# Both mixers of a two-layer encoder: the order of gate chunks, pooled maps and decay sums rearranged

## The chip, the cores and the metric

One core of one Trainium2 chip runs the kernel. The metric is the device time of one execution in microseconds; the number that is predicted is the median over several runs.

## What is computed

Two layers, 256 tokens of width 1024, all in float32. Each layer has a mixer, an output projection, a layer norm, a channel mixer (dense SwiGLU in layer 0; top 2 of 8 experts in layer 1) and a second norm. The part that the change touches is the mixer, cut here to what matters:

```python
z = x @ w_in                     # pool 512 | q 512 | k 512 | v 512 | o 512 | gates 8
y_pool = pool_mixer(u_pool, ...) # trailing means over 2, 4, 8, 16 tokens minus the token; a 128x128 map per group
q, k = causal_conv_silu(qk)      # 4 taps
Dlog = b[t] - b[s] + ig[s]       # causal; b = cumsum(log_sigmoid(f))
m_t  = max(max_s Dlog, inter)
W    = exp(Dlog - m_t) * (q . k) * Dh**-0.5
num  = W @ v ;  den = sum_s W
h    = num / max(|den|, exp(-m_t))
h    = (h - mean) * rsqrt(var + eps)       # per head
y_m  = sigmoid(o_pre) * h * g
mix  = concat(y_pool, y_m) @ w_out
x    = layer_norm(ALPHA * x + mix)
```

The kernel computes the four heads over all 256 tokens at once, without the reference's chunks of 64.

## The kernel before

TensorE's exactness is bought by splitting. Each weight unit of 128x2048 (1 MB) arrives in `raw` by a DMA of SP's queue, ScalarE rounds it to float32r (`w_hi`, four buffers, `round_hi`, L824), VectorE subtracts (`w_lo`, three buffers, `subtract_lo`, L1172), and each product is three float32r matmuls, high by high, high by low and low by high (`product`, L1739 to L1741). Small matmuls (scores, sums, maps, transposes) are plain float32; the profile shows each such matmul as two records. A mixer has 14 units: v0 v1 q0 q1 k0 k1 p0 p1 o0 o1 (halves of the input projection, p for pool and o for the output gate) and w0 to w3 (`w_out`). Units of the mixer are numbered u0 to u13 here in that order. A helper called `ahead()` stands between the steps of ScalarE and of VectorE and does the next unit there; unit n can only be rounded when TensorE is through with unit n-4 and subtracted when it is through with unit n-3.

The order of each engine is written out by hand; nothing reorders it.

- TensorE (`mixer`, L1772 on): values, gates, chunks of q, of k, transposes of the gate rows (L1837), four broadcasts of the row of maxima to 128 partitions (L1840: a selector of 4x128 against `r_negm` of 4x256), p0 and p1, the scores (L1852 and L1853), o0, then the row sums of the decay weights W as matmuls with a column of ones (L1863, 12 matmuls of one column), the products of W with v (L1868, 12 matmuls of 128 columns; called PV here), pooled maps 0 and 1 (`pool_maps(0)`, L1877), o1, a wait for all four sigmoids, `pool_maps(1)` (L1877 again), `project(0, 0)` and `project(0, 1)` (the first quarter of the output projection for tokens 0 to 127 and 128 to 255; 12 matmuls of 512 columns each), eight transposes of the normed heads (L1913), and the other quarters for the first tokens and then for the second.
- The scores wait for all arguments of the exponentials (`arg_ready`), since their banks hold the broadcasts until then. PV waits for `w_ready`, four masked and multiplied W.
- ScalarE (L858 on): bias and gate functions, copies of q and k to SBUF (L874), eight SiLUs (L885), four exponentials (L907), `guard` (L909), u10, the four copies of the pool chunks to `ubuf` (L915), u11, u12 (which waits for the end of o0), rounding of the pooled outputs (`y_round`, L920), sigmoids of o (L926), standard deviations (L929).
- VectorE (L1201 on): v copies, the gate rows, convolutions (L1247, L1249), arguments of the exponentials (L1277, L1278), u9 has its subtraction here, then u10, then the four products W (L1286), u11, denominators (L1295 to L1299), `pooled(0)` (L1305), `head_stats(0)`, `y_low(0)`, `head_stats(1)`, `pooled(1)`, the two normings with a reciprocal each (L1344, L1346), `y_low(1)`, u12, eight products with the sigmoids (L1355), `y_low(2)` (L1316), u13, `y_low(3)`.
- GpSimd, called POOL: two of the eight convolutions, the causal mask on the exponentials (`masks`, L776), then the pooling of groups 0 to 3 (`pooling`, L733 to L749: g0 to g3 here).
- PSUM banks: pool and gate chunks use 0 to 3, so a chunk of o0 may start when ScalarE has copied the pool chunk out of its bank. PV uses banks 7 and 6, the sums 4; the projection sums into 0, 1, 4 and 5.

The lines of the code stand here as the profile counts them.

Of the kernel before, what the change touches and what calls it, by code (L numbers as in the profile page):

```python
# [7 lines left out]
F32 = mybir.dt.float32  # L8
# [205 lines left out]
def build(nc, x, w_in, b_gates, conv_w, conv_b, pool_w, pool_scale, mlstm_g, w_out, ln1_g, ln1_b, ln2_g, ln2_b,  # L214
          wg_dense, wu_dense, wd_dense, w_router, b_router, wg_exp, wu_exp, wd_exp, consts, out):
    with ExitStack() as ctx:
# [42 lines left out]
        def carve(shape, start=None):  # L259
            if start is not None:  # L260
# [23 lines left out]
        v_sb = carve([TT, D_MLSTM])  # L284
# [9 lines left out]
        rows = carve([5, T])  # L294
        qkT = carve([8, T])
        yT = qkT
        r_i, r_f, r_l, r_negm, r_m = (rows[0:HEADS, n, :] for n in range(5))
# [107 lines left out]
            ypool_ready, rden_ready, hvar_ready, h_ready, ym_ready, ylo_ready, var_ready, xhat_ready, dh_ready, \  # L405
# [3 lines left out]
                "cols_ready", "arg_ready", "w_ready", "ypool_ready", "rden_ready", "hvar_ready", "h_ready",  # L409
# [8 lines left out]
        shift_ready, turn_go = map(sem, ("shift_ready", "turn_go"))  # L418
# [36 lines left out]
        PV_BANKS = (7, 6)  # L455
        POOL_BANKS = (5, 2)
# [242 lines left out]
        def _(pool):  # L699
# [31 lines left out]
            def pooling(l):  # L731

                st.then(g.memset(ptmp[:, :, 0:16], 0.0))  # L733
                for gr in range(GROUPS):
# [45 lines left out]
            for l in range(LAYERS):  # L780
                convs(l)
                masks(l)
                pooling(l)
# [12 lines left out]
        def _(act):  # L796
# [61 lines left out]
            def mixer(l):  # L858
# [31 lines left out]
                copies("q", 0)  # L890
                if l:
                    act.wait_ge(tokens_ready, TT * 2)
# [11 lines left out]
                silu(3)  # L904
                for h in range(HEADS):
# [243 lines left out]
        def _(dve):  # L1149
# [51 lines left out]
            def mixer(l):  # L1201
                ahead()
                for t in range(TT):
                    dve.wait_ge(*chunk_event(l, "v", t))
                    v.tensor_copy(v_sb[:, t, :], bank[t][:, :]).then_inc(v_ready, 1)
# [22 lines left out]
                st.add(v.tensor_scalar(r_negm, r_m, -1.0, None, ALU.mult))  # L1228
                st.wait()
# [62 lines left out]
                dve.wait_ge(pv_mm, TT * l + 1)  # L1292
                den = bank[4][:, 0:TT * HEADS]
                rd, gd = (w[:].rearrange("p t h -> p (t h)") for w in (rden, guard))
                st.then(v.tensor_tensor(rd, den, gd, ALU.max))  # L1295
# [1009 lines left out]
```

## Time and profile before

| | before |
|---|---|
| median of 3 runs | 1341.83 us (1340.31 to 1342.46) |
| the profiled execution | 1338.05 us |
| its span | 1336.2 us |
| PE busy | 1278.6 us (96%) |
| PE weight load busy | 1044.5 us (78%) |
| DVE busy | 1126.5 us (84%) |
| ACT busy | 928.8 us (70%) |
| POOL busy | 89.3 us (7%) |
| mean granted clock of PE | 0.984 |

PE is TensorE, DVE is VectorE, ACT is ScalarE, POOL is GpSimd, SP is SyncE, which issues the weight loads. All times inside a trace count from the start of its span. The granted clock is a share of 2.4 GHz. The busy time of matmuls overlaps with the next one's (they are pipelined), so the distance from one start to the next says more than the length of one. The first mixer lies at 12 to 110 us, the dense part behind it up to about 310 us, the second mixer at 310 to 410 us, the routing of the experts at 410 to 440 us, and the experts behind it.

### The profile page before, as it was taken

How to read it: one execution, taken by the hardware profiler on the slowest of the kernel's cores; microseconds unless marked ns; L12 is line 12 of the kernel's file. 1: busy time of each engine (PE TensorE's matmuls, PEld its weight loads, DVE VectorE, ACT ScalarE, POOL GpSimd, SP SyncE). 2: the span in 40 equal slices, each digit the busy share in tenths (PEclk: the TensorE clock that was granted, in tenths of full speed). 3: DMA queues.
4: the chain of work that ended last, by engine and by line, in shares of the span. 5: the costliest groups of instructions: out<-in, count | busy, mean ns of one | idle time of the engine just before them, and what ended most of it. 6: DMA issues, size and time to landing. Idle time of an engine off the chain costs nothing.

```text
span 1336.2 us, 17022 instructions
## 1 busy us (share of the span) xinstructions
PE 1278.6 (96%) x6176; PEld 1044.5 (78%) x6176; DVE 1126.5 (84%) x931; ACT 928.8 (70%) x745; POOL 89.3 (7%) x111
## 2 busy tenths in 40 slices
PE   7999999999997989999999999999999999999996
PEld 5997888888986768777877777777777787677774
DVE  5868644458968799999998999879899989899997
ACT  5645444445534688888886888878778888788883
POOL 1550000000740000000000000000000000000000
PEclk9999999999996999999999999999999999999998
DMA  9637555544442999999999999999999999999992
GB/s 321 217 105 247 193 188 189 190 157 158 157 142 81 345 377 387 389 400 403 409 408 409 389 410 395 407 399 409 347 367 408 396 409 409 409 399 393 398 406 105
DMA packets 133053, 425.18 MB, mean 318 GB/s; under 512 B 9008, under 2 KB 11344, under 8 KB 132960
## 3 DMA queue, kind: packets, MB, share of 16 engines
q1 hardware_dynamic: 131600, 420.21, 82.8%
q0 software_dynamic: 1216, 3.71, 0.9%
q8 instruction: 53, 0.87, 0.3%
q14 instruction: 40, 0.33, 0.1%
q10 hardware_dynamic: 144, 0.07, 0.0%
HBM read 422.91 MB, written 1.05 MB: 317 GB/s over the span
## 4 chain that ended last, share of the span: by engine, by line
PE 76%; DVE 14%; issue 6%; ACT 3%; DMA 0%; DVEq 0%; ACTq 0%
PE bank L1739 19%; PE bank L1741 18%; PE bank L1740 18%; DVE w_lo L1158 7%; PE bank L2060 6%; PE bank L2061 6%; DVE w_lo L1172 2%; PE bank L2106 1%; PE bank L2093 1%; PE bank L2019 1%; PE bank L2034 1%; PE bank L2056 1%; PE bank L2057 1%; ACT w_hi L824 1%; DVE arena L1249 1%
## 5 line engine op out<-in xcount | busy, mean ns | idle before, releaser
L1158 DVE TENSOR_TENSOR w_lo<-raw,w_hi 128x2048 fp32r<-128x2048 f32 x216 | 485.9, 2285 | 32.8 <-PE bank L1741 18.8
L809 ACT CAST w_hi<-raw 128x2048 fp32r<-128x2048 f32 x216 | 407.5, 1915 | 67.8 <-PE bank L1741 66.6
L1739 PE MATMUL bank<-w_hi,parts 128*128 128x512 f32 x824 | 330.3, 401 | 13.5 <-issue 5.7
L1741 PE MATMUL bank<-w_hi,parts 128*128 128x512 f32 x824 | 322.7, 392 | 0.0
L1740 PE MATMUL bank<-w_lo,parts 128*128 128x512 f32 x824 | 322.4, 391 | 0.0
L2060 PE MATMUL bank<-w_hi,parts 128*128 128x512 f32 x672 | 270.0, 402 | 9.0 <-ACT arena L1024 3.1
L2061 PE MATMUL bank<-w_lo,parts 128*128 128x512 f32 x672 | 262.5, 391 | 0.0
L1739 PEld LDWEIGHTS bank<-w_hi,parts 128*128 128x128 f32 x824 | 155.6, 189 | 55.9 <-issue 15.2
L1172 DVE TENSOR_TENSOR w_lo<-raw,w_hi 128x2048 fp32r<-128x2048 f32 x61 | 140.3, 2303 | 62.7 <-PE bank L1741 51.7
L1158 DVE TENSOR_TENSOR w_lo<-arena,w_hi 128x2048 fp32r<-128x2048 f32 x80 | 181.2, 2285 | 10.6 <-ACT w_hi L809 8.5
L1741 PEld LDWEIGHTS bank<-w_hi,parts 128*128 128x128 f32 x824 | 155.5, 189 | 33.5
L1740 PEld LDWEIGHTS bank<-w_lo,parts 128*128 128x128 f32 x824 | 155.9, 189 | 30.9 <-issue 0.7
L824 ACT CAST w_hi<-raw 128x2048 fp32r<-128x2048 f32 x61 | 116.2, 1910 | 80.6 <-PE bank L1741 72.0
L2060 PEld LDWEIGHTS bank<-w_hi,parts 128*128 128x128 f32 x672 | 126.1, 188 | 53.9 <-DVE w_lo L1158 23.0
L809 ACT CAST w_hi<-arena 128x2048 fp32r<-128x2048 f32 x80 | 150.9, 1913 | 16.1 <-PE bank L2061 12.5
L2061 PEld LDWEIGHTS bank<-w_lo,parts 128*128 128x128 f32 x672 | 126.3, 188 | 25.1 <-issue 0.7
L1158 DVE TENSOR_TENSOR w_lo<-tokens,w_hi 128x2048 fp32r<-128x2048 f32 x40 | 91.4, 2285 | 2.8 <-ACT w_hi L809 2.3
L1739 PE MATMUL bank<-w_hi,x_hi 128*128 128x512 f32 (+1 forms) x224 | 85.3, 381 | 4.1 <-DVE w_lo L1172 4.0
L1741 PE MATMUL bank<-w_hi,x_lo 128*128 128x512 f32 (+1 forms) x224 | 84.8, 378 | 0.0
L1740 PE MATMUL bank<-w_lo,x_hi 128*128 128x512 f32 (+1 forms) x224 | 84.7, 378 | 0.0
L809 ACT CAST w_hi<-tokens 128x2048 fp32r<-128x2048 f32 x40 | 76.9, 1923 | 6.0 <-issue 4.3
L1739 PE MATMUL bank<-x_hi,w_hi 128*128 128x256 f32 x256 | 73.4, 287 | 0.4 <-ACT arena L915 0.4
(251 smaller groups left out, 1267.1 us busy)
## 6 DMA issues: line engine op xcount, KB each, us to landing
raw<-in_wu_exp SPq DMA_DIRECT2D x76, 1024.0 KB, 10.2
raw<-in_wg_exp SPq DMA_DIRECT2D x70, 1024.0 KB, 10.2
raw<-in_wd_exp SPq DMA_DIRECT2D x70, 1024.0 KB, 10.6
arena<-in_wd_exp SPq DMA_DIRECT2D x29, 1024.0 KB, 10.6
arena<-in_wg_exp SPq DMA_DIRECT2D x26, 1024.0 KB, 11.2
arena<-in_wu_exp SPq DMA_DIRECT2D x25, 1024.0 KB, 8.8
raw<-in_w_in SPq DMA_DIRECT2D x20, 1024.0 KB, 5.9
tokens<-in_wg_exp SPq DMA_DIRECT2D x16, 1024.0 KB, 11.8
```

What stands on the lines that cost most here:

```text
L809: a.copy(to, ring[s]).then_inc(hi_ready, 1)
L824: a.copy(w_hi[:, n % HIGH, :], raw[:, n % RAW, :]).then_inc(hi_ready, 1)
L1158: v.tensor_tensor(low(n), ring[s], high(n).bitcast(F32), ALU.subtract).then_inc(lo_ready, 1)
L1172: v.tensor_tensor(w_lo[:, n % SPLIT, :], raw[:, n % RAW, :], w_hi[:, n % HIGH, :].bitcast(F32), ALU.subtract).then_inc(lo_ready, 1)
L1249: ins = v.scalar_tensor_tensor(out=acc, in0=zqk[:, c, j:j + T], scalar=par_col(("conv_w", j), l, c), in1=acc, op0=ALU.mult, op1=ALU.add)
L1739: mm(psum, left[0], right[0], start=first, stop=False)
L1740: mm(psum, left[0], right[1], start=False, stop=False)
L1741: return mm(psum, left[1], right[0], start=False, stop=last)
L2019: last = mm(psum[:, at_c:at_c + width], parts_[:, t, k * P:(k + 1) * P], picks[:, t, :], start=t == 0, stop=t == TT - 1)
L2034: last = mm(bank[n][:, kk * BOTH:(kk + 1) * BOTH], parts_[:, t, k * P:(k + 1) * P], pick_both[:, t, :], start=t == 0, stop=t == TT - 1)
L2060: mm(psum, left, right[0], start=first, stop=False)
L2061: return mm(psum, left, right[1], start=False, stop=last)
```

## The change

Six edits, all in the mixers, in both layers.

1. The column of ones goes into `v_sb`: each head's v is 129 columns wide, the last one ones. The 12 one-column matmuls (L1863) are gone; the 12 PV matmuls have 129 columns and give sums beside the products. Three heads of a token tile lie in bank 7 or 6, the fourth head of both tiles in bank 4 (`head_sums`). The denominators are now read from three places, so their two VectorE operations become six, and they wait for all of PV. The wait of the projection for `rden_ready` becomes one for `hvar_ready`, put ahead of `project(0, 1)`.
2. The negated maxima are written as two float32r rows (`negm_hi`, `negm_lo`) with one more VectorE operation; the broadcast is two float32r matmuls for each head instead of one float32 matmul. ScalarE rounds the selector once (`head_sel`) in layer 0, after the copies of q.
3. TensorE runs chunks 0 and 1 of o0 before the scores, chunks 2 and 3 after them.
4. ScalarE copies pool chunks 0 to 2 before the exponentials, the last one after `guard`, and u10 comes after that one.
5. POOL runs g0 before the masks, g1 to g3 after them.
6. TensorE runs `pool_maps(1)` between `project(0, 0)` and `project(0, 1)`, and VectorE runs `pooled(1)` between the two normings instead of before both.

```diff
@@ buffers
-        v_sb = carve([TT, D_MLSTM])
+        v_sb = carve([TT, HEADS, DH + 1])
...
-        rows = carve([5, T])
+        rows = carve([4, T])
...
+        head_sel = parts[0:HEADS, 4096:4096 + HEADS * P]
+        negm_hi, negm_lo = (parts[0:HEADS, 4096 + HEADS * P + n * T:][:, 0:T] for n in range(2))
...
+        def head_sums(t, h):
+            b, c = (PV_BANKS[t], h) if h < HEADS - 1 else (4, t)
+            return bank[b][:, c * (DH + 1):(c + 1) * (DH + 1)]
@@ GpSimd
                 convs(l)
+                pooling(l, range(0, 1))
                 masks(l)
-                pooling(l)
+                pooling(l, range(1, GROUPS))
@@ ScalarE
                 copies("q", 0)
+                if l == 0:
+                    act.wait_ge(consts_in, 16)
+                    a.copy(head_sel, cst[0:HEADS, C_SEL:C_SEL + HEADS * P]).then_inc(sel_ready, 1)
...
                 silu(3)
+                act.wait_ge(qk_ready, 8 * (l + 1))
+                for c in range(GROUPS - 1):
+                    pool_input(c)
                 for h in range(HEADS):
                     act.wait_ge(arg_ready, HEADS * l + h + 1)
                     a.activation(decay[:, h, :], decay[:, h, :], ACT.Exp).then_inc(decay_ready, 1)
...
+                pool_input(GROUPS - 1)
                 ahead()
-                act.wait_ge(qk_ready, 8 * (l + 1))
-                for c in range(GROUPS):
-                    act.wait_ge(*chunk_event(l, "p", c))
-                    a.copy(ubuf[:, c, 16:], bank[c][:, 0:T]).then_inc(u_ready, 1)
                 ahead()
                 ahead()
@@ VectorE
+                    if t == 0:
+                        v.memset(v_sb[:, :, :, DH:DH + 1], 1.0).then_inc(vones_ready, 1)
...
-                st.add(v.tensor_scalar(r_negm, r_m, -1.0, None, ALU.mult))
-                st.wait()
+                st.then(v.tensor_scalar(negm_hi, r_m, -1.0, None, ALU.mult))
+                st.then(v.scalar_tensor_tensor(out=negm_lo, in0=r_m, scalar=-1.0, in1=negm_hi.bitcast(F32),
+                                               op0=ALU.mult, op1=ALU.subtract))
...
-                dve.wait_ge(pv_mm, TT * l + 1)
-                den = bank[4][:, 0:TT * HEADS]
...
+                dve.wait_ge(pv_mm, TT * (l + 1))
...
+                for rd_, gd, den in dens:
+                    st.add(v.tensor_tensor(rd_, den, gd, ALU.max))
+                st.wait()
+                for rd_, gd, den in dens:
+                    st.add(v.scalar_tensor_tensor(out=rd_, in0=den, scalar=-1.0, in1=rd_, op0=ALU.mult, op1=ALU.max))
+                st.wait()
...
                 head_stats(1)
-                pooled(1)
                 for t in range(TT):
...
+                    if t == 0:
+                        pooled(1)
@@ TensorE
+                pe.wait_ge(sel_ready, 1)
                 pe.wait_ge(rows_ready, l + 1)
...
-                    last = mm(bank[(7, 4)[h // 2]][:, (h % 2) * T:(h % 2 + 1) * T],
-                              cst[0:HEADS, C_SEL + h * P:C_SEL + (h + 1) * P], r_negm, start=True, stop=True)
+                    row = bank[(7, 4)[h // 2]][:, (h % 2) * T:(h % 2 + 1) * T]
+                    mm(row, head_sel[:, h * P:(h + 1) * P], negm_hi, start=True, stop=False)
+                    last = mm(row, head_sel[:, h * P:(h + 1) * P], negm_lo, start=False, stop=True)
...
                 chunks("p", 1)
+                chunks("o", 0, lambda c: (u_ready, GROUPS * l + c + 1), range(0, 2))
...
-                chunks("o", 0, lambda c: (u_ready, GROUPS * l + c + 1))
+                chunks("o", 0, lambda c: (u_ready, GROUPS * l + c + 1), range(2, 4))
...
-                for t in range(TT):
-                    for h in range(HEADS):
-                        for w, s in wts[t][h]:
-                            mm(bank[4][:, t * HEADS + h:t * HEADS + h + 1], w, ones[:, 0:1],
-                               start=s == 0, stop=s == t)
...
-                            last = mm(bank[PV_BANKS[t]][:, h * DH:(h + 1) * DH], w, v_sb[:, s, h * DH:(h + 1) * DH],
-                                      start=s == 0, stop=s == t)
+                            last = mm(head_sums(t, h), w, v_sb[:, s, h, :], start=s == 0, stop=s == t)
...
                 pe.wait_ge(sig_ready, HEADS * (l + 1))
-                pool_maps(1)
...
-                pe.wait_ge(rden_ready, l + 1)
                 arrived(mixer_unit(l, "w", 0))
                 project(0, 0)
+                pool_maps(1)
                 pe.wait_ge(ypool_ready, 2 * l + 1)
+                pe.wait_ge(hvar_ready, TT * (l + 1))
                 project(0, 1)
```

## Rows read from the trace of the kernel before

**Rows 1.** The page's part 4: the chain that ended last, shares of the span by engine.

```profile
PE 76%; DVE 14%; issue 6%; ACT 3%; DMA 0%; DVEq 0%; ACTq 0%
```

**Rows 2.** PE in stretches: bounds, length, busy (instructions), granted clock, DMA share, GB/s.

```profile
56.20:67.70 11.50, 11.50 (x96) 1.00 0.28 93
...
110.00:320.00 210.00, 206.43 (x998) 1.00 0.56 184
...
500.00:800.00 300.00, 295.64 (x1315) 1.00 1.02 400
```

**Rows 3.** PE timeline, first mixer: start us, us, engine, line, output<-inputs, count [idle<-releaser].

```profile
54.23 1.97 PE L1840 MATMUL bank<-arena,cst 4*128 4x256 f32 x8
...
67.75 0.59 PE L1852 MATMUL bank<-arena 128*128 128x256 f32 x2
...
76.11 2.74 PE L1863 MATMUL bank<-cst,arena 128*128 128x1 f32 x24
...
78.71 4.55 PE L1868 MATMUL bank<-arena 128*128 128x128 f32 x24
...
83.10 1.03 PE L1877 MATMUL bank<-arena,pool_ws 128*128 128x256 f32 x4
...
90.35 1.13 PE L1877 MATMUL bank<-arena,pool_ws 128*128 128x256 f32 x4 [0.47 <-ACT arena L926]
...
100.49 0.47 PE L1739 MATMUL bank<-w_hi,parts 128*128 128x512 f32 x1
```

**Rows 4.** PE timeline, second mixer, the same columns.

```profile
361.05 0.67 PE L1852 MATMUL bank<-arena 128*128 128x256 f32 x2 [1.67 <-DVE arena L1278]
...
377.09 1.03 PE L1877 MATMUL bank<-arena,pool_ws 128*128 128x256 f32 x4
```

**Rows 5.** PE in short stretches, columns of Rows 2.

```profile
78.00:79.00 1.00, 1.00 (x10) 1.00 0.03 8
...
80.00:81.00 1.00, 1.00 (x6) 0.50 0.73 119
...
26.50:30.00 3.50, 3.50 (x33) 1.00 1.05 390
...
414.00:418.00 4.00, 2.97 (x13) 0.52 0.01 2
```

**Rows 6.** DVE timeline, both mixers, columns of Rows 3.

```profile
65.33 2.29 DVE L1172 TENSOR_TENSOR w_lo<-raw,w_hi 128x2048 fp32r<-128x2048 f32 x1
...
68.55 2.29 DVE L1172 TENSOR_TENSOR w_lo<-raw,w_hi 128x2048 fp32r<-128x2048 f32 x1 [0.94 <-ACT w_hi L824]
...
70.77 1.94 DVE L1286 SCALAR_TENSOR_TENSOR arena<-bank,arena 128x384 f32<-128x384 f32 x4
...
91.52 0.88 DVE L1305 TENSOR_SCALAR arena<-bank,par 128x256 f32<-128x256 f32 x2 [0.84 <-PE bank L1877]
...
360.81 2.28 DVE L1172 TENSOR_TENSOR w_lo<-raw,w_hi 128x2048 fp32r<-128x2048 f32 x1
```

**Rows 7.** ACT timeline, both mixers, the same columns.

```profile
63.56 1.28 ACT L907 ACT_TABLE_LOAD   x1
...
64.85 1.76 ACT L907 ACTIVATE arena<-arena 128x384 f32<-128x384 f32 x4
...
68.42 1.17 ACT L915 COPY arena<-bank 128x256 f32<-128x256 f32 x4
...
358.00 0.91 ACT L885 ACTIVATE arena<-arena,par 128x256 f32<-128x256 f32 x2 [1.82 <-DVE arena L1249]
```

**Rows 8.** POOL timeline, first mixer, the same columns.

```profile
66.75 1.94 POOL L776 TENSOR_SCALAR_AFFINE_SELECT arena<-arena 128x512 f32<-128x512 f32 x2 [5.49 <-ACT arena L907]
...
69.10 2.22 POOL L744 TENSOR_TENSOR arena<-arena 128x256 f32<-128x256 f32 x1
...
73.54 1.31 POOL L744 TENSOR_TENSOR arena<-arena 128x256 f32<-128x256 f32 x2
...
76.02 0.72 POOL L749 TENSOR_TENSOR arena<-arena 128x256 f32<-128x256 f32 x1
```

More of the change, by code:

```diff
@@ L293, in build @@
         ln_rows = {1: ln_old, 2: ln_mid, 3: ln_new}
-        rows = carve([5, T])
+        rows = carve([4, T])
         qkT = carve([8, T])
         yT = qkT
-        r_i, r_f, r_l, r_negm, r_m = (rows[0:HEADS, n, :] for n in range(5))
+        r_i, r_f, r_l, r_m = (rows[0:HEADS, n, :] for n in range(4))
+        head_sel = parts[0:HEADS, 4096:4096 + HEADS * P]
+        negm_hi, negm_lo = (parts[0:HEADS, 4096 + HEADS * P + n * T:][:, 0:T] for n in range(2))
         y_hi, y_lo = (shaped(parts[:, n * 2048:(n + 1) * 2048], [8, T]) for n in range(2))
@@ L729, in _, with pooling @@
             st = Steps(pool, pool_steps)
-            def pooling(l):
-                st.then(g.memset(ptmp[:, :, 0:16], 0.0))
-                for gr in range(GROUPS):
+            def pooling(l, groups):
+                if 0 in groups:
+                    pool.wait_ge(u_ready, GROUPS * l + 1)
+                    st.then(g.memset(ptmp[:, :, 0:16], 0.0))
+                for gr in groups:
                     pool.wait_ge(u_ready, GROUPS * l + gr + 1)
@@ L1291, in mixer @@
                 dve.wait_ge(guard_ready, l + 1)
-                dve.wait_ge(pv_mm, TT * l + 1)
-                den = bank[4][:, 0:TT * HEADS]
-                rd, gd = (w[:].rearrange("p t h -> p (t h)") for w in (rden, guard))
-                st.then(v.tensor_tensor(rd, den, gd, ALU.max))
-                v.scalar_tensor_tensor(out=rd, in0=den, scalar=-1.0, in1=rd, op0=ALU.mult, op1=ALU.max) \
-                    .then_inc(rden_ready, 1)
-                dve.wait_ge(rden_ready, l + 1)
+                dve.wait_ge(pv_mm, TT * (l + 1))
+                rd = rden[:].rearrange("p t h -> p (t h)")
+                most = HEADS - 1
+                of_t = [bank[PV_BANKS[t]][:, 0:most * (DH + 1)].rearrange("p (h d) -> p h d", h=most)[:, :, DH]
+                        for t in range(TT)]
+                of_last = bank[4][:, 0:TT * (DH + 1)].rearrange("p (t d) -> p t d", t=TT)[:, :, DH]
+                dens = [(rden[:, t, 0:most], guard[:, t, 0:most], of_t[t]) for t in range(TT)] \
+                    + [(rden[:, :, most], guard[:, :, most], of_last)]
+                for rd_, gd, den in dens:
[4 more added lines that the diff above has]
+                st.wait()
                 st.then(v.reciprocal(rd, rd))
@@ L1772, in mixer, with chunks @@
             def mixer(l):
-                def chunks(kind, half, free=None):
-                    arrived(mixer_unit(l, kind, half))
+                def chunks(kind, half, free=None, cs=range(4)):
+                    if 0 in cs:
+                        arrived(mixer_unit(l, kind, half))
                     hi, lo = parts_of(mixer_unit(l, kind, half), FBLK)
-                    for c in range(4):
+                    for c in cs:
                         if half == 0 and free is not None:
@@ L1859, in mixer @@
                       [[(decay[:, h, P:T], 0), (decay[:, h, T:T + P], 1)] for h in range(HEADS)]
+                pe.wait_ge(vones_ready, l + 1)
                 for t in range(TT):
```

14 lines of the change are left out of this document (9 added, 5 removed).

## The prediction

> **What bounds the kernel now.** I read the chain that ended last first: three quarters of it are TensorE [rows 1]. Outside the mixers TensorE is all but full, 206.4 of 210 us in the dense part and 295.6 of 300 in a stretch of the experts [rows 2], so time won in a mixer should shift everything behind it by the same amount. Then the timeline of TensorE through the two mixers, because every edit sits there. The reader is to see three things. The p block is full: 96 products in 11.5 us, 0.120 us from one to the next [rows 2]. The 24 one-column records take 2.60 us (76.11 to 78.71), as much as their weight loads, and PV behind them 4.39 us (78.71 to 83.10) for 24 records [rows 3]. And the scores of the second mixer wait 1.67 us for VectorE [rows 4]. Last the granted clock by the microsecond: 1.00 at 78 us, 0.50 at 80 us, in the middle of PV [rows 5]. The level is 1.2 instead of 2.4 GHz; what TensorE did before it fell was the one-column matmuls. A run of 128-column float32 records at 26.5 us kept the clock at 1.00 [rows 5], and there 33 records took 3.5 us, 0.106 each; at that rate PV would take 2.6 us. So 1.8 us of PV is the lower clock. Then ScalarE, VectorE and POOL over the same stretch, since they decide what is late once TensorE is faster.
>
> **Broadcasts (edit 2).** Eight float32 records took 1.97 us with the p block starting at 56.20 [rows 3]; eight float32r matmuls of 256 columns at the products' 0.120 take 0.96. With some 0.1 for the change of type I take 0.8 off, and p starts at 55.4. The rounding of the selector is 512 elements on four partitions, about 0.6 us of ScalarE once (an exponential of 384 elements takes 0.44 [rows 7]), ahead of a SiLU that has slack; taken as nothing, at most 0.6 if that cover is gone. VectorE gets one more operation of 256 elements on the gate rows, 0.45 us by its neighbours of the same shape (bounds 0.3 to 0.5 from the 256-element operations of Rows 7 and 6). In the first mixer it vanishes in waits; in the second VectorE runs without a gap up to the arguments, so their end moves from 360.8 [rows 6] to 361.25, and the last SiLU from 358.9 [rows 7] to 359.35.
>
> **Ones column (edit 1).** Minus 2.60 us, minus 1.8 if the clock stays up; the one more column per matmul is under 0.1 us in all. Bounds for PV: 2.6 us (full clock) and 4.4 (as now); I take 2.65, since what preceded the fall is gone and the 26.5 us row is its nearest kin. The v copies write rows of 129 instead of 128 elements: nothing. The denominators need three or four more tiny VectorE operations, 0.4 us, and now start after all of PV; VectorE is then waiting for the pooled map anyway, which hides them.
>
> **Order around the scores (edits 3 and 4), first mixer.** TensorE's own path: p ends at 66.9, two chunks of o (24 products) 2.9, to 69.8, scores 2.6 (67.75 to 70.3 now [rows 3]), to 72.4, two chunks 2.9, to 75.35. What PV waits for is the other chain, and this is where a wait appears. ScalarE's SiLUs end at 63.54; copies 0 and 1 are free; copy 2 needs pool chunk 2, done 1.4 us before p ends, at 65.65 with its latency, so it ends at 66.0. Table load 1.28, exponentials 1.7 [rows 7]: 69.0, against 66.6 now. Guard and copy 3: 69.4. The rounding of u10, 1.9 long, is queued behind: 71.3. VectorE's u10 (its two predecessors 2.29 each, 2.22 from start to start) follows at 73.5 instead of 70.8, and W, 1.9 [rows 6], at 75.45. PV starts at 75.55: 0.2 us of wait, where W was ready 3.4 us ahead before.
>
> **The same, second mixer.** The scores' wait went from 359.4 to 361.05 [rows 4]. Now p ends at 358.35 and chunk o0 needs copy 0, which follows the last SiLU: 359.8, so 1.5 us of idle comes back in another place. Then 2.9 + 2.6 + 2.9 = 8.4, to 368.2. ScalarE: three copies (0.29 each back to back [rows 7], 0.38 with the waits), table load, exponentials, guard, copy 3, u10: 365.8; VectorE u10 and W: 370.0. PV starts at 370.1, after 1.8 us of wait.
>
> **POOL (edit 5).** g0 starts at 64 us (359.8), runs into VectorE's subtraction of u9 (65.33 and 360.81, 2.3 long [rows 6]) and ends at 69.2 (about 365.2); the masks need the exponentials at 69.0 (363.5) anyway and end at 71.2 (367.2), ahead of VectorE's use. That an add takes 2.22 us when it meets VectorE's u10 (68.55 to 70.84) and 0.65 when alone is in the rows: 69.10 against two in 1.31 [rows 8]. Then g1, 3.5 us alone (73.28 to 76.74), starts at 71.2 into the subtraction of u10 and ends into that of u11, which follows W directly: 71.2 + 2.3 + 3.2 + 2.3 = 79.0. In the second mixer 367.3 + 0.8 + 3.4 + 2.2 = 373.7. Now g1 is done long before `pool_maps(0)`; after the change PV ends at 78.2 and 372.75, so TensorE waits 0.9 us in each mixer. Bounds: nothing (POOL's step wins over u11) to 2.3 (one more collision).
>
> The Trainium skill (SBUF — State Buffer, Who interferes with whom) says that a VectorE instruction with two SBUF inputs and a POOL instruction that reads SBUF exclude each other and that the later one waits in full. The 2.22 us add agrees; the masks, 1.94 us beside u9 [rows 8], don't show it. By the rule held strictly, the masks too would wait for u10, and PV would come up to 1 us later than in my sum.
>
> **Gain up to the start of `pool_maps(0)`.** First mixer 83.10 to 79.1, minus 4.0; second 377.09 to 373.7, minus 3.4.
>
> **Maps 1 moved (edit 6).** The wait for four sigmoids stays (0.47 [rows 3]). Now `pool_maps(1)` at 90.35 releases `pooled(1)` at 91.52 [rows 6], and from there VectorE does pooled, both normings, y_low(1), u12, eight products, y_low(2), which lets TensorE go on with the second quarter at 100.49 [rows 3]: 8.97 us. TensorE's own work from 90.35 is 9.9 us, so the two are level to 0.3 us. After: the map comes behind `project(0, 0)`, 12 products at 0.227 (24 of them and the maps lie between 90.35 and the transposes at 96.8), so `pooled(1)` starts 2.9 us later against the maps' old place, and only the first norming (1.25 us) has been taken out of the chain behind it. What is late next is VectorE: 2.9 - 1.25 - 0.15 of slack = 1.5 us of new wait for TensorE before the second quarter. g3 is done at about 88.7, the map needs it at 89.2: hidden. I give 1.5 in each mixer; bounds 0 and 1.8.
>
> **Sum.** First mixer -4.0 + 1.5 = -2.5, second -3.4 + 1.5 = -1.9, together -4.4 us. The profiled execution (1338.05 us, span 1336.2) would be 1333.6; the median stands 3.8 above the profiled one, and 1341.83 - 4.4 = 1337.4.
>
> **Rivals.** *The waits don't form* (chance 0.2): u10, u11 and POOL fit better than I place them, and the maps' chain costs nothing. For it: each wait is under 2 us and worked out from starts good to some 0.3. Against it: the queue order is fixed. Then -4.4 - 3.0 - 0.2 = -7.6: 1334.2.
> *The clock falls all the same* (0.2): PV then takes 4.4 instead of 2.65 or the half speed lies over maps and o1, 1.8 us a mixer: -4.4 + 3.6 = -0.8, 1341.0; in one mixer only, 1339.2. For it: idle of 0.2 to 1.8 us on either side of PV. Against: the 1.67 us wait now costs no clock. The Trainium skill (TensorE: Matmul & The Clock Gate, HAM oscillation) blames idle gaps between bursts; by that the new waits around PV would do it, while the row at 80 us shows a fall behind full, thin matmuls with no gap.
> *Saved time isn't passed on* (0.07): the dense part's 3.6 idle us in 210 [rows 2] grow because the weights' rounding, not TensorE, is the pace; the first mixer's 2.5 goes: -1.9, 1339.9.
> *Slower* (0.08): the clock falls in PV of a mixer and stays at 0.50 through maps, o1 and the projections, as it stayed low at 414 to 418 us (0.52) behind idle time [rows 5]. PV to the transposes is 15.4 us of work at full clock (2.65 + 0.7 + 5.8 + 0.8 + 5.5), so one mixer pays 15.4: +11, 1352.8. It decides against the change from 7.1 us of half-speed work more than forecast.
>
> **Chances.** The forecast has 0.45. A measurement of this kernel tells about 0.2% (2.7 us) from no change. Faster by more: forecast and first rival, 0.65, less a little for the forecast's edge and plus the one-mixer case: 0.64. Within: 0.26. Slower: 0.10. The range takes the first rival whole with the bound of 1.8 instead of 1.5 and a microsecond for the median's own scatter (1340.3 to 1342.5), and the clock's rival at its top: 1332.5 to 1341.5; the slower case is left out.
>
> **What would show it.** No one-column records; PV in 2.65 us at clock 1.00 (if it is longer, look at the clock row); broadcasts under 1.1 us; TensorE idle before o0 in the second mixer (1.5), before PV released by VectorE's W (0.2 and 1.8), before `pool_maps(0)` released by POOL (0.9 each), and before the second quarter released by y_low(2) (1.5 each); the dense and expert stretches shifted, not stretched. The prediction is wrong if VectorE is not the one that ends last before the second quarter, or if POOL's collisions with the subtractions fall elsewhere.

## The result, and the profile after

| | before | after |
|---|---|---|
| median | 1342.14 us (4 runs, 1340.31 to 1343.52) | 1333.70 us (4 runs, 1332.11 to 1334.92) |
| ratio | | 0.9945, 95% interval 0.9927 to 0.9963 |
| the same kernel again, another set of runs | 1340.04 us (9 runs) | 1332.00 us (5 runs), 0.9938, interval 0.9924 to 0.9951 |
| profiled execution and its span | 1338.05, 1336.2 | 1332.11, 1330.3 |

The kernel is 8.0 to 8.4 us faster in the medians, 5.9 in the two profiled executions. The forecast was 1337.4, range 1332.5 to 1341.5. The result lies in the range, 3.7 us below the forecast and 0.5 below the first rival's 1334.2.

The head of the page after and its chain of work (part 4): TensorE has 48 records fewer (24 in each mixer, the thin matmuls), and VectorE holds one per cent more of the chain.

```profile
span 1330.3 us, 16942 instructions
PE 1269.6 (95%) x6128; PEld 1035.7 (78%) x6128; DVE 1128.5 (85%) x943; ACT 929.9 (70%) x746; POOL 91.3 (7%) x111
...
PE 74%; DVE 15%; issue 7%; ACT 4%; DMA 0%; DVEq 0%; ACTq 0%
```

Timeline of TensorE after, first mixer (start us, us, engine, line, output<-inputs, count, [idle<-releaser]). The last row is the norm's first transposes, where the mixer hands over; before they started at 110.11.

```profile
55.36 0.39 PE L1770 MATMUL bank<-x_hi,w_hi 128*128 128x256 f32 x1
...
75.64 2.95 PE L1899 MATMUL bank<-arena 128*128 128x129 f32 x24
...
78.43 0.60 PE L1907 MATMUL bank<-arena,pool_ws 128*128 128x256 f32 x2
...
85.67 0.50 PE L1770 MATMUL bank<-w_hi,parts 128*128 128x512 f32 x1 [0.47 <-ACT arena L945]
...
97.35 0.47 PE L1770 MATMUL bank<-w_hi,parts 128*128 128x512 f32 x1 [1.38 <-DVE parts L1346]
...
106.97 0.49 PE L1790 MATMUL bank<-cst,work 128*128 128x128 f32 x3
```

Second mixer, the same columns. The last row belongs to the second half's norm, the last one ahead of the routing. Before, it started at 414.20.

```profile
356.99 0.36 PE L1770 MATMUL bank<-x_hi,w_hi 128*128 128x256 f32 x1 [1.41 <-ACT arena L922]
...
366.88 2.95 PE L1899 MATMUL bank<-arena 128*128 128x129 f32 x24 [1.30 <-DVE arena L1309]
...
369.66 0.60 PE L1907 MATMUL bank<-arena,pool_ws 128*128 128x256 f32 x2
...
388.58 0.47 PE L1770 MATMUL bank<-w_hi,parts 128*128 128x512 f32 x1 [1.38 <-DVE parts L1346]
...
408.28 1.68 PE L1790 MATMUL bank<-cst,work 128*128 128x128 f32 x8 [3.12 <-DVE work L1410]
```

TensorE in stretches, after (bounds, length, busy (instructions), granted clock, DMA share, GB/s). The first row lies in PV.

```profile
77.00:78.00 1.00, 1.00 (x12) 1.00 1.04 408
...
110.00:320.00 210.00, 206.32 (x1005) 1.00 0.56 185
500.00:800.00 300.00, 295.64 (x1318) 1.00 1.02 399
```

The one-column records are gone. PV takes 75.64 to 78.43, 2.79 us, at clock 1.00, where sums and PV together took 6.99 in [rows 3], partly at 0.50 [rows 5]. The first mixer hands over 3.14 us sooner (110.11 to 106.97); at the last norm it is 5.92 (414.20 to 408.28), so the second mixer gave 2.8. From there to the end of the span it is 922.0 us in both kernels (1336.2 - 414.20, 1330.3 - 408.28): the difference between the two profiled executions is made in the mixers. That the two agree to 0.1 us is chance: in the ten profiled executions of the experiments below this stretch takes 920.3 to 924.2 us. The dense stretch and the experts' stretch are those of [rows 2].

### The profile page after: what moved, and what is told of

Same layout as the page of the kernel before. It is cut to its first block, busy times and chain, and to the rows that moved or that the text cites. A ratio compares the mean times of both kernels' runs of the same rounds, so it can differ in the third digit from the quotient of the medians.

```text
span 1330.3 us, 16942 instructions
## 1 busy us (share of the span) xinstructions
PE 1269.6 (95%) x6128; PEld 1035.7 (78%) x6128; DVE 1128.5 (85%) x943; ACT 929.9 (70%) x746; POOL 91.3 (7%) x111
## 4 chain that ended last, share of the span: by engine, by line
PE 74%; DVE 15%; issue 7%; ACT 4%; DMA 0%; DVEq 0%; ACTq 0%
PE bank L1770 18%; PE bank L1772 18%; PE bank L1771 18%; DVE w_lo L1177 8%; PE bank L2090 6%; PE bank L2091 6%; DVE w_lo L1191 2%; PE bank L2136 1%; ACT w_hi L836 1%; PE bank L2123 1%; PE bank L2049 1%; PE bank L2064 1%; PE bank L2086 1%; PE bank L2087 1%; DVE arena L1272 1%
## 5 line engine op out<-in xcount | busy, mean ns | idle before, releaser
L821 ACT CAST w_hi<-raw 128x2048 fp32r<-128x2048 f32 x216 | 407.5, 1915 | 66.1 <-PE bank L1772 65.0
## 6 DMA issues: line engine op xcount, KB each, us to landing
raw<-in_wu_exp SPq DMA_DIRECT2D x76, 1024.0 KB, 11.2
```

Of the source, the lines that this page charges most:

```text
L821: a.copy(to, ring[s]).then_inc(hi_ready, 1)
```

## The experiments

"Turn 1" is the start of the norm's first transposes in layer 0, "turn 2" the same in the second mixer, "last turn" the row shown above at 408.28. All are TensorE starts in one profiled execution of each kernel, so a clock that falls or doesn't moves them. The ratio is of medians against the kernel before in the same set of runs. Each diff shows the lines that matter, not the whole edit.

In the dense part between the two mixers the clock also fell in some of these executions: once in e0, e6 and e8, twice in e5 and e7, never in the others. One such fall costs about 1.5 us of the last two columns (an estimate from after and e0_after, the same kernel: 301.31 and 302.82 us from turn 1 to the last turn, see the end of this section).

| kernel | median (runs) | ratio, 95% interval | turn 1 | turn 2 | last turn |
|---|---|---|---|---|---|
| before | | | 110.11 | 404.11 | 414.20 |
| after | 1333.70 (4) | 0.9945, 0.9927 to 0.9963 | 106.97 | 398.19 | 408.28 |
| e0_after | 1332.00 (5) | 0.9938, 0.9924 to 0.9951 | 106.67 | 399.40 | 409.49 |
| e1_ones_only | 1335.29 (4) | 0.9958, 0.9941 to 0.9974 | 107.66 | 400.63 | 410.72 |
| e8_broadcast_only | 1339.51 (11) | 0.9983, 0.9973 to 0.9992 | 108.94 | 404.61 | 414.69 |
| e2_map_back | 1334.42 (4) | 0.9943, 0.9927 to 0.9960 | 108.09 | 401.35 | 411.43 |
| e4_old_order | 1334.57 (4) | 0.9946, 0.9929 to 0.9962 | 106.72 | 400.81 | 410.89 |
| e3_thin_again | 1343.28 (10) | 1.0016, 1.0003 to 1.0030 | 111.25 | 408.34 | 418.42 |
| e5_fill_wait | 1333.61 (5) | 0.9951, 0.9937 to 0.9964 | 107.01 | 401.38 | 411.54 |
| e6_u10_first | 1332.36 (5) | 0.9939, 0.9926 to 0.9953 | 107.66 | 400.16 | 410.24 |
| e7_all_three | 1334.01 (5) | 0.9949, 0.9934 to 0.9963 | 106.69 | 400.20 | 410.37 |
| e9_u10_masks | 1339.65 (11) | 0.9982, 0.9970 to 0.9994 | 108.90 | 404.94 | 415.02 |

The medians of before were 1341.01 (13 runs) beside e1 to e4, 1340.04 (9) beside e0 and e5 to e7, and 1341.45 (21) beside e8 and e9.

### The first edit alone

The kernel before with edit 1 and nothing else.

```diff
-                            mm(bank[4][:, t * HEADS + h:t * HEADS + h + 1], w, ones[:, 0:1],
-                               start=s == 0, stop=s == t)
...
-                            last = mm(bank[PV_BANKS[t]][:, h * DH:(h + 1) * DH], w, v_sb[:, s, h * DH:(h + 1) * DH],
+                            last = mm(head_sums(t, h), w, v_sb[:, s, h, :],
```

> The kernel before with the column of ones alone (edit 1). Theory A (POOL is next in line): PV follows o0 directly and at full clock, so the second map is wanted 4.2 us sooner, at 86.1 us, but POOL ends its last group at 87.8 as before; TensorE waits 1.7 us there and the second quarter of the projection starts at 98.0 instead of 100.49. In the second mixer POOL's last group ends 0.3 us ahead of the map already, so nearly nothing more is won. Span 1333.4 (-2.8). Theory B (TensorE's time counts in full, POOL is never late): -4.2 in each mixer, span 1327.8. Both: PV 2.8 us at clock 1.00.

Measured: 5.7 us off the median, two thirds of what all six edits bring. The span is 1331.0, between the two theories. Theory A's wait for POOL ahead of the second map came in the first mixer, 1.74 us where it said 1.7; in the second mixer, where it expected nearly none, there are two. Its timeline of TensorE shows what the saved time ran into, in the second mixer here:

```profile
371.89 0.70 PE L1887 MATMUL bank<-arena,pool_ws 128*128 128x256 f32 x2 [1.00 <-POOL arena L754]
378.81 0.70 PE L1887 MATMUL bank<-arena,pool_ws 128*128 128x256 f32 x2 [0.47 <-ACT arena L931]
381.31 0.70 PE L1887 MATMUL bank<-arena,pool_ws 128*128 128x256 f32 x2 [1.80 <-POOL arena L754]
```

POOL's groups, which had slack before, come last for both maps once PV is short. The profiled execution also had 0.50 at 346 to 349 us, 0.8 us behind the start of the p block and so behind the eight float32 broadcasts, which are still there in this kernel; whether they are the cause wasn't tested.

### The second edit alone

The kernel before with edit 2 and nothing else.

```diff
-                    last = mm(bank[(7, 4)[h // 2]][:, (h % 2) * T:(h % 2 + 1) * T],
-                              cst[0:HEADS, C_SEL + h * P:C_SEL + (h + 1) * P], r_negm, start=True, stop=True)
+                    mm(row, head_sel[:, h * P:(h + 1) * P], negm_hi, start=True, stop=False)
+                    last = mm(row, head_sel[:, h * P:(h + 1) * P], negm_lo, start=False, stop=True)
```

> The kernel before with edit 2 alone. Both theories expect the four broadcasts to end within 1.1 us instead of 1.97, the p block to start 0.8 us sooner, and in the second mixer the scores to wait 1.67 + 0.8 + 0.45 = 2.9 us for VectorE, since the row of maxima costs it one more operation. Theory A (an idle stretch of 2.9 us costs only itself): the norm's turn of the second mixer starts at 414.20 - 0.5 + 0.1 = 413.8, the median is that of before within 1 us. Theory B (it brings the granted clock down as in the kernel with the old order, where a wait of 2.98 us ahead of the scores was followed by 6 us at 0.50): scores and first o chunks run at half speed, the turn starts at about 416, the median is 1.5 to 2.5 us longer than before.

Measured: 1.9 us off the median, while its profiled execution is 0.5 us late at the last turn (0.50 at 309 to 312 us, where before had 1.00, is in it). Theory A's details hold but for size: the broadcasts took 1.13 us (53.91 to 55.04), the scores of the second mixer waited 2.39 us, not 2.9, and the median moved by 1.9 us where it allowed 1.

```profile
78.40 2.92 PE L1876 MATMUL bank<-arena 128*128 128x128 f32 x24
...
361.54 0.67 PE L1860 MATMUL bank<-arena 128*128 128x256 f32 x2 [2.39 <-DVE arena L1284]
```

In stretches, the same kernel: the thin matmuls and PV of the first mixer, then the stretch behind the wait.

```profile
79.00:81.00 2.00, 2.00 (x20) 1.00 0.67 164
...
362.00:364.00 2.00, 2.00 (x13) 1.00 0.00 0
```

Theory B falls in this execution: the clock stays at 1.00 behind an idle stretch of 2.39 us. And PV in the first mixer took 2.76 us at 1.00 although the thin matmuls were there. In the second mixer it fell as before (0.50 at 375 and 376 us). So the fall behind the thin matmuls is frequent and not certain, and a median over runs and one profile can't agree to a microsecond here. The medians of the two kernels add up: 5.7 + 1.9 = 7.6 of 8.0 to 8.4. What edits 3 to 6 add is within the scatter. A kernel with edits 1 and 2 together and nothing else was not run, so this is a sum of two runs and not a measurement.

### The thin matmuls put back

The kernel after, with 12 matmuls of one column that nobody reads ahead of PV.

```diff
+                            mm(bank[4][:, 300 + t * HEADS + h:301 + t * HEADS + h], w, ones[:, 0:1],
+                               start=s == 0, stop=s == t)
```

> The changed kernel with the 12 one-column matmuls put back ahead of PV, into columns of bank 4 that nobody reads: their result is not used. Theory A (the thin matmuls bring the clock down): they take 2.6 us a mixer, the granted clock falls to 0.50 in PV or the maps and costs 1.8 more: span 1330.3 + 8.8 = 1339.1. Theory B (the clock fell for another reason that the change also removed): clock stays at 1.00, span 1335.5.

Measured: 1343.28, slower than before; the last turn 10.1 us later than after's. Timeline of TensorE, both mixers:

```profile
75.61 2.84 PE L1899 MATMUL bank<-cst,arena 128*128 128x1 f32 x24 [0.17 <-DVE arena L1309]
78.31 4.57 PE L1904 MATMUL bank<-arena 128*128 128x129 f32 x24
...
371.04 4.06 PE L1899 MATMUL bank<-cst,arena 128*128 128x1 f32 x24 [1.29 <-DVE arena L1309]
374.96 4.97 PE L1904 MATMUL bank<-arena 128*128 128x129 f32 x24
```

In stretches, the same kernel, both mixers:

```profile
78.00:79.00 1.00, 1.00 (x10) 0.93 0.25 86
80.00:81.00 1.00, 1.00 (x7) 0.50 0.90 322
...
373.00:374.00 1.00, 1.00 (x6) 0.50 0.70 287
```

The wait ahead of them is 0.17 us in the first mixer, and there is no gap inside the group, yet the clock is 0.50 at 80 us. PV takes 4.4 and 4.8 us with the thin matmuls ahead and 2.8 without. Theory A is confirmed, with the fall in the second mixer longer than it said: it began inside the thin group, which took 3.9 instead of 2.7. The span is 1342.6 where theory A had 1339.1: 1.3 us of that lie in the mixers, and 2.2 behind the last turn, where this execution takes 924.2 us instead of 922.0; why is open. Over all kernels here, PV ran partly at half speed in five of the six mixers that have the thin group (before, e3 and e8), and in none of the 18 that don't (after, e0, e1, e2, e4 to e7 and e9: the group is 2.85 to 2.95 us long in each).

### The map back in its place

The kernel after, edit 6 undone.

```diff
                 pe.wait_ge(sig_ready, HEADS * (l + 1))
+                pool_maps(1)
...
                 project(0, 0)
-                pool_maps(1)
```

On VectorE `pooled(1)` goes back ahead of both normings.

> The changed kernel with its second map back behind the sigmoids and the pooled scaling ahead of both normings (edit 6 undone). Theory A (the move buys off POOL's lateness at the price of a wait for VectorE of 1.4): TensorE waits for POOL's last group (done at 87.5 and 379.3), 2.0 and 2.6 us, and the wait of 1.38 us ahead of the second quarter is gone; second quarter at 97.8 (+0.4) and 390.0 (+1.4); span 1331.7. Theory B (as I put it in the prediction: POOL is in time and the move costs 1.4 a mixer): span 1327.5.

Measured: 1334.42, the last turn 3.15 us later than after's, where 1.4 was expected. The median can't tell it from after. The rows show what edit 6 buys, and that this execution lost more than its waits:

```profile
85.41 0.70 PE L1906 MATMUL bank<-arena,pool_ws 128*128 128x256 f32 x2 [0.47 <-ACT arena L945]
87.25 0.70 PE L1906 MATMUL bank<-arena,pool_ws 128*128 128x256 f32 x2 [1.14 <-POOL arena L760]
```

```profile
86.00:87.00 1.00, 0.11 (x1) 1.00 0.00 0
88.00:89.00 1.00, 1.00 (x4) 0.50 0.00 0
```

In its old place the second half of map 1 waits for POOL's g3 (1.14 us here, 1.74 in the second mixer), and in both mixers the clock falls to 0.50 right behind (also 382 to 384 us) and lies over `project(0, 0)`. The 1.38 of wait before the second quarter is absent; `project(0, 0)` at half speed gives VectorE more time there, so whether the wait would be absent at full clock isn't shown. So edit 6 trades a wait for POOL for one of about the same length for VectorE; what more it is worth in this pair is the clock. That fall is not certain either: e1 has longer waits in the same place (0.47 and 1.74 us, 0.47 and 1.80) and keeps the clock at 1.00 behind them.

### The old order around the scores

The kernel after, edits 3, 4 and 5 undone.

```diff
                 chunks("p", 1)
-                chunks("o", 0, lambda c: (u_ready, GROUPS * l + c + 1), range(0, 2))
...
-                chunks("o", 0, lambda c: (u_ready, GROUPS * l + c + 1), range(2, 4))
+                chunks("o", 0, lambda c: (u_ready, GROUPS * l + c + 1))
```

> The changed kernel with the order around the scores of before (edits 3, 4 and 5 undone; ones column, split maxima and the moved map kept). Theory A (these edits only shift waits from the scores to o0 and to W, and give POOL an earlier end): first mixer the same within 0.4 us; second mixer: scores wait 3 us for the arguments instead of 1.4 + 1.3 in two places, and POOL's last group comes 1 us late for the map: span 1331.5 (+1.2). Theory B (the early pool copies and half of o0 ahead of the scores carry much of the gain): +3 or more, span over 1333.

Measured: 1334.57, the last turn 2.6 us later. Nothing is lost in the first mixer (turn 1 at 106.72, against 106.97). The second, timeline and stretches of TensorE:

```profile
358.19 1.19 PE L1884 MATMUL bank<-arena 128*128 128x256 f32 x2 [2.98 <-DVE arena L1299]
```

```profile
358.00:360.00 2.00, 1.80 (x5) 0.50 0.00 0
362.00:364.00 2.00, 2.00 (x9) 0.50 0.92 365
```

With the broadcasts faster and VectorE's row one operation longer, the scores wait 2.98 us, and the clock is at 0.50 behind it until 364 us. The moved chunks of o are what fills that gap. In the one layer where it exists the order is worth, in this execution, the clock; the idle time itself is 2.98 us against 1.41 and 1.30 in after. e8 had the same wait 0.6 us shorter and kept the clock. The span, 1332.6, lies between the theories. Theory A's wait for the arguments came as it said; its late last group of POOL didn't, for in this kernel no map waits for POOL. The three edits were undone together, so the run doesn't price any one of them.

### Filling the waits before the second quarter

The kernel after, with quarter 1 run for both halves ahead of quarters 2 and 3 of the first.

```diff
-                for t in range(TT):
-                    for q in range(1, 4):
+                for q, t in ((1, 0), (1, 1), (2, 0), (3, 0), (2, 1), (3, 1)):
```

> The changed kernel with TensorE's order of the projection quarters (1,0) (1,1) (2,0) (3,0) (2,1) (3,1) instead of (1,0) (2,0) (3,0) (1,1) (2,1) (3,1), so that a quarter that needs nothing new covers the wait for VectorE's third split. Theory A (that wait, 1.38 us a mixer, is the price of the moved map and VectorE is late by just that): the wait goes in both mixers, -2.8 us against the changed kernel. Theory B (VectorE is the bound of the whole tail, so the wait comes back ahead of the later quarters or of the norm): within 0.5 us of the changed kernel.

Measured: 1333.61, no gain. The wait of 1.38 is gone and one of 1.77 stands ahead of the norm:

```profile
107.01 1.09 PE L1790 MATMUL bank<-cst,work 128*128 128x128 f32 x8 [1.77 <-DVE work L1410]
```

VectorE's first residual (L1399) starts at 102.56 instead of 101.72, as TensorE finishes the first half's sums later. Turn 1 is at 107.01 against 106.97. So the wait came back ahead of the norm, as theory B said. That VectorE bounds the whole tail is not shown by it, for VectorE idles 2.79 us for TensorE ahead of that residual (1.71 in after).

In the code the norm's transposes stand in the middle of quarter 2 of the second half. From the first residual to that place TensorE has 5.25 us of work in after (101.72 to 106.97) and 2.68 here (102.56 to 105.24), since quarter 1 of the second half has moved ahead of the residual; from the residual to the norm it takes 4.45 us (102.56 to 107.01). The new order took away what covered this chain. An order that fills the wait and puts the transposes later was not run, so the 1.38 us may still be there to be won.

### Pulling u10 forward, and both together

e6: the kernel after, u10 rounded ahead of the exponentials.

```diff
                 for c in range(GROUPS - 1):
                     pool_input(c)
+                ahead()
                 for h in range(HEADS):
...
                 pool_input(GROUPS - 1)
-                ahead()
```

> The changed kernel with ScalarE's rounding of u10 ahead of the exponentials instead of behind the last pool copy. Theory A (the wait ahead of PV is the chain exponentials, copy, u10, its subtraction, W): the subtraction runs beside the exponentials and masks, W is ready 1.3 us sooner in the second mixer, and PV follows o0 without a wait: -1.5 us in all. Theory B (masks and pooling on POOL run into the subtraction and are as late): no gain, or up to 1 us lost at the maps.

Measured: 1332.36, not to be told from after. PV waits 1.03 us in both mixers (0.1 and 1.30 in after). VectorE and then POOL in the first mixer:

```profile
66.99 4.49 DVE L1191 TENSOR_TENSOR w_lo<-raw,w_hi 128x2048 fp32r<-128x2048 f32 x2
74.31 1.95 DVE L1309 SCALAR_TENSOR_TENSOR arena<-bank,arena 128x384 f32<-128x384 f32 x4 [2.83 <-POOL arena L787]
```

```profile
67.00 5.15 POOL L759 TENSOR_SCALAR arena<-arena 128x240 f32<-128x240 f32 x1
...
73.05 1.23 POOL L787 TENSOR_SCALAR_AFFINE_SELECT arena<-arena 128x512 f32<-128x512 f32 x2
```

u9 and u10 now run back to back, and one small POOL operation of g0 (0.82 us when alone) lasts 5.15 us across both. The masks stand behind it in POOL's queue, and W waits for the masks. Theory B.

e7 is e5 and e6 together, with `project(0, 0)` waiting for two sigmoids instead of four.

```diff
-                pe.wait_ge(sig_ready, HEADS * (l + 1))
+                pe.wait_ge(sig_ready, HEADS * l + 2)
...
                 project(0, 0)
+                pe.wait_ge(sig_ready, HEADS * (l + 1))
                 pool_maps(1)
```

> The changed kernel with both edits of the two runs before and the first quarter of the projection started after two sigmoids instead of four (the others are waited for ahead of the second map). Theory A: -2.8 - 1.5 - 0.9 = -5.2 us against the changed kernel, -12.6 against the one before. Theory B (VectorE bounds the tail): -1.5 us at most against the changed kernel.

Measured: 1334.01. PV waits 0.56 and 1.04, the norm 1.77 and 1.80 <- L1410. Turn 1 at 106.69. No gain: the waits ahead of the norm are those of e5, and the order of the quarters is e5's too.

e9 is e6 with edit 5 undone (masks ahead of g0), to free W from the blocked g0.

```diff
-                pooling(l, range(0, 1))
                 masks(l)
-                pooling(l, range(1, GROUPS))
+                pooling(l, range(GROUPS))
```

> The kernel after, with u10 rounded ahead of the exponentials and with edit 5 undone (masks ahead of group 0). Theory A (POOL's blocked group 0 is what made W late when u10 alone was moved): the masks end within 1.5 us of the last exponential, PV waits under 0.3 us in the first mixer and under 0.6 in the second instead of 1.03 twice; groups 0 and 1, 4.3 us alone, then start at about 72.5 and run into u11's subtraction, so that the maps wait 0 to 1.0 us for POOL; the norm's turn of the second mixer starts at 407.5 to 409, against 408.28. Theory B (the two subtractions in a row keep VectorE itself from W): PV waits 1.0 us in both mixers as before, the turn starts at 410 or later.

Measured: 1339.65, most of the gain gone. Theory A on PV: no wait in the first mixer, 0.38 in the second. But the maps wait much longer than its 0 to 1.0, and the last turn is at 415.02, not at 407.5 to 409:

```profile
80.65 0.70 PE L1906 MATMUL bank<-arena,pool_ws 128*128 128x256 f32 x2 [2.08 <-POOL arena L760]
...
374.04 1.22 PE L1906 MATMUL bank<-arena,pool_ws 128*128 128x256 f32 x2 [2.75 <-POOL arena L760]
```

POOL in the first mixer, and VectorE's u11, which starts at the same time:

```profile
75.47 3.23 POOL L755 TENSOR_TENSOR arena<-arena 128x256 f32<-128x256 f32 x2
```

```profile
75.56 2.67 DVE L1190 TENSOR_TENSOR w_lo<-raw,w_hi 128x2048 fp32r<-128x2048 f32 x1 [1.27 <-PE bank L1771]
```

```profile
376.00:379.00 3.00, 3.00 (x16) 0.50 0.01 3
```

g1's adds start at 75.47, 0.09 us ahead of u11; the first gets through and the second is held until u11 is done. In after the adds are over by then. In the second mixer it is g0's last operation that starts 0.20 us behind u11 (367.81 and 367.61) and takes 2.66 us instead of 0.74. And the clock (last row, stretches of TensorE) is at 0.50 there from the wait ahead of the map to 380 us, over most of o1. This is the collision that the prediction put into the kernel after, made to happen. It is also the clearest case for edit 5: e6 and e9 differ by it alone, and g0 behind the masks makes the maps 2 us and more late and the last turn 4.8 us (410.24 to 415.02), the clock's fall over o1 included. Both have u10 pulled forward; in the kernel after itself edit 5 was not undone alone.

### The same kernel once more

The kernel after, unchanged.

> The changed kernel once more, on the chip of the next three. All theories: 7 to 8 us under the kernel before; waits of 0.2 and 1.3 us ahead of PV and of 1.4 us ahead of the second quarter in both mixers.

Its profiled execution has the same waits in the mixers as the first one (1.41, 1.28, 1.38, 1.38), and one thing that the first hadn't, in the dense part. TensorE in stretches, first this execution, then the first one of after:

```profile
117.00:118.00 1.00, 0.55 (x2) 0.97 0.00 0
119.00:121.00 2.00, 2.00 (x6) 0.50 0.94 339
```

```profile
118.00:121.00 3.00, 3.00 (x14) 1.00 0.70 196
```

In both TensorE idles about 2 us in two waits just ahead (0.65 and 1.20 here, 0.75 and 1.20 there). Once the clock fell behind them, once it didn't. All four profiled executions of this set of runs (e0, e5, e6, e7) fall at this place and none of the six others that have the two waits (after, e1, e2, e4, e8, e9) does, so what decides it may be something that differs between the sets; it is open. From turn 1 to the last turn this execution takes 302.82 us, the first one 301.31.

## Why the prediction was right, and where not

**What bounds it, and that savings pass through.** Right. The last 922.0 us are the same in both profiles, within the 920.3 to 924.2 that the others show. The rival of a gain that isn't passed on fell.

**Broadcasts.** p starts at 55.36, forecast 55.4. The extra VectorE operation made the scores late in the second mixer, as worked out (2.39 in e8, 2.98 in e4, from 1.67).

**Ones column.** PV at 2.79, taken at 2.65, clock 1.00. That thin matmuls bring the clock down was read from [rows 5] alone; e3 shows it. The rival that the clock falls all the same didn't come in the kernel after: it stays at 1.00 through both of its mixers up to the last norm. In PV it didn't come in any of the nine kernels without the thin matmuls. Over the maps and what follows them it did come in two, behind waits for POOL: in e2 behind map 1, in e9 over map 0 and o1 of the second mixer.

**The waits ahead of PV.** First mixer 75.64, forecast 75.55. Second: 1.41 before o0 (forecast 1.5) and 1.30 before PV (forecast 1.8).

**`pool_maps(0)` waits 0.9 us for POOL.** This step failed, and it is one of the forecast's own signs of being wrong, that POOL's collisions fall elsewhere. There was no wait in the first mixer and none that the trace shows in the second. POOL after, first mixer, then its last operation of g1 in the second:

```profile
69.54 1.22 POOL L787 TENSOR_SCALAR_AFFINE_SELECT arena<-arena 128x512 f32<-128x512 f32 x2
...
70.97 3.23 POOL L755 TENSOR_TENSOR arena<-arena 128x256 f32<-128x256 f32 x2
...
75.37 0.73 POOL L760 TENSOR_TENSOR arena<-arena 128x256 f32<-128x256 f32 x1
...
367.29 2.31 POOL L760 TENSOR_TENSOR arena<-arena 128x256 f32<-128x256 f32 x1
```

VectorE after, first mixer, the same stretch:

```profile
71.38 2.35 DVE L1191 TENSOR_TENSOR w_lo<-raw,w_hi 128x2048 fp32r<-128x2048 f32 x1 [3.40 <-ACT w_hi L836]
73.65 1.94 DVE L1309 SCALAR_TENSOR_TENSOR arena<-bank,arena 128x384 f32<-128x384 f32 x4
75.61 2.63 DVE L1191 TENSOR_TENSOR w_lo<-raw,w_hi 128x2048 fp32r<-128x2048 f32 x1
```

In the first mixer two sizes and one order were off. The masks took 1.22 us, not the 1.94 of [rows 8]: there they ran beside u9, here in a stretch where VectorE has no subtraction. Of g1, the first add had already started when u10 began, and 2.4 us were left at the end of u10 (73.73 to 76.10), not 3.2. And g1's last operation starts at 75.37, 0.24 us ahead of u11 at 75.61, so here VectorE is the later one: u11 takes 2.63 us instead of 2.29, and POOL loses nothing, where the forecast had g1 run into u11 and end at 79.0. The forecast had named this as its lower bound. In the second mixer the forecast's collision took place and was shorter: 3.06 us of g1 were left behind u10 (not 3.4) and u11 cost 1.58 (2.31 instead of 0.73, not 2.2), so g1 ends at 369.60, just as PV ends. The forecast's mechanism is real (e9: 2.08 and 2.75); in the first mixer its place depended on a quarter of a microsecond.

The Trainium skill (SBUF — State Buffer, Who interferes with whom) says that the later of the two instructions waits in full. The adds and the 5.15 us of e6 agree. The masks agree too, against the reading of [rows 8] in the forecast. The two masks of the first mixer before, one by one (shortest, median and longest in ns, first and last start in us):

```profile
L776 POOL TENSOR_SCALAR_AFFINE_SELECT arena<-arena x2: 624/990/1355, 66.8 to 68.1; 128x512 f32<-128x512 f32 x2
```

The first, from 66.75, takes 1.355 us and ends 0.49 us behind u9 (65.33 + 2.29 = 67.62); the second, with no subtraction beside it, takes 0.624. The operations that are held end in the same way: the add of [rows 8] and the one of g1 in after end 0.48 and 0.47 us behind the subtraction, against 0.61 alone. So 1.94 is one mask held by u9 and one free, not two slowed ones.

**Map 1.** The wait before the second quarter came as 1.38 in both mixers, forecast 1.5, behind y_low(2). But the forecast took the maps' old place as one in which map 1 waits for nothing but the sigmoids. That held for the kernel before only. With PV short, the old place waits for POOL (1.74 and 1.80 in e1, 1.14 and 1.74 in e2). g3 was "hidden" only because the map had moved. So 1.5 was right as a term of the sum and wrong as a price of edit 6, which by the medians costs nothing against undoing it.

**The sum.** Forecast for the profiled execution -4.4 (first mixer -2.5, second -1.9), measured -5.9 (-3.1, -2.8). Without the two waits of 0.9 for POOL the forecast's own terms give -6.2; the 0.3 between are the small misses of the other terms.

**The first rival.** The median lies 0.5 us from its 1334.2, but that is luck. Its words were that none of the waits forms; five of the seven did (before PV 0.1 and 1.30 us, before o0 1.41, before the second quarter 1.38 twice; only POOL's two are missing). Nor is its number the price of its words: it takes off the 3.0 of the maps' chain and 0.2. With the 1.8 before PV in the second mixer and the two waits of 0.9 for POOL off as well, the forecast's own terms give -11.2, 1330.6. The profiled pair gained 5.9, not 7.6; the rest came between the profiled execution and the median.

**From the profiled execution to the median.** The forecast took 3.8 us between them for both kernels. For after it was 1.6 in the first set, and in the second the profiled execution was the slowest of five. This is where the other 2 us come from. Over 43 executions of before in the three sets, the mean span is 1339.4 at a mean clock of 0.9811, so the profiled one (1336.2 at 0.984) was one of the fastest; over nine of after the mean is 1331.2 at 0.9847. Among the 43, 0.001 more of clock goes with 0.68 us less of span, so the difference of 0.0036 would be 2.4 us of the 8.3, of which the profiled pair (0.984 and 0.986) has 1.4. That gives about 1 us of the missing 2.4 to the clock and leaves the rest open: the clock is given to three digits, and only one execution of before has a trace. Nor is that clock a matter of luck alone, since the change itself keeps it up in PV.

## What to carry to other kernels

In this kernel a row of thin matmuls cost 2.6 us and, in five mixers of six, half speed for what came next; a column of ones in the operand that is multiplied anyway cost next to nothing (PV at full clock takes 2.79 us with 129 columns, 2.76 with 128 in e8). When an edit shortens TensorE's path, price the old order of the *new* kernel too, since engines that had slack (POOL here) come last in it. A collision that hangs on a fraction of a microsecond should stand as a rival with both ends, not as a term of the sum.

## What the runs showed of the hardware that was not expected

- A POOL operation of 0.82 us that meets two VectorE subtractions in a row is held across both, 5.15 us (e6). The masks are 1.22 us with no subtraction beside them and 1.94 us [rows 8] when the first of the two is held by one. Which of the two engines waits goes by who starts first: 0.24 us decided it in after.
- The granted clock fell to 0.50 behind thin float32 matmuls without a gap (e3) and in one execution less than 1 us behind float32 broadcasts of four rows (e1; the kernel before has the same broadcasts and kept 1.00). Behind idle time of 2.98 us (e4) and 2.75 us (e9) it fell, behind 2.39 us (e8) it didn't, and behind two waits of about 1.9 us together it did in one execution of the kernel after and not in another. Behind 0.47 and 1.14 us it fell (e2), behind 0.47 and 1.74 in the same place it didn't (e1). The Trainium skill (TensorE: Matmul & The Clock Gate, HAM oscillation) names idle gaps as the cause; e4 and e9 agree, e3 has a cause that is not among them, and e1, e2 and e8 show that the length of the gap alone doesn't decide it here.
